# The output projection of a two-layer decoder trunk, split by rows and threaded between the attention heads

## The reference

```python
D_MODEL, SEQ, DEPTH = 2048, 512, 2          # batch 1
# layer 0: S5 state-space mixer (1024) | FoX attention, 8 heads of 128 | memory attention, 4 heads
# layer 1: latent attention MLA, 8 heads | sparse attention NSA, 8 heads | memory attention, 4 heads
for layer in range(DEPTH):
    xn = rms_norm(h, norm_g[layer])
    mem_kv = mem_n @ mem_w_kv[layer]
    mixed = even_layer(xn, mem_kv, ...) if layer % 2 == 0 else odd_layer(xn, mem_kv, ...)
    h = h + (mixed @ w_out[layer]).astype(h.dtype)      # (512, 2560) @ (2560, 2048)
return rms_norm(h, final_norm_g)

# attention, per head: s = q k^T * scale (+ bias); p = softmax(s); o = p v; y = o * silu(gate)
# NSA, per head: three softmaxes (selected 512 keys, window 512 keys, compressed 31 keys),
#   each weighted by its own sigmoid gate, their outputs summed
```

## Time and profile before

| | |
|---|---|
| three executions | 2541.16, 2548.64, 2548.69 us |
| profiled execution, its span | 2541.77 us, 2540.2 us |
| PE, busy | 2366.3 us (93%), 11912 matmuls |
| DVE, ACT, POOL, busy | 1009.8, 831.7, 348.4 us (40%, 33%, 14%) |
| chain that ended last | PE 86%, DVE 5%, issue 3%, DMA 2%, ACT 2% |
| OUT0, OUT1 | 1021.0 to 1240.4 us, 2292.9 to 2512.9 us |
| FOX, MEM0 | 908.5 to 979, 979 to 1021 us |
| MLA, NSA, MEM1 | 2000.6 to 2093, 2103.2 to 2245.3, 2245.3 to 2292.9 us |

### The profile page before, as it was taken

The page is one execution under the profiler, slowest core; times in us unless marked ns, Lnnn a source line. Parts: engine busy times, 40 slices in busy tenths (PEclk is TensorE's granted clock), DMA queues, the critical chain, the costliest instruction groups (busy, mean ns, idle before and its releaser), DMA issues.

```text
span 2540.2 us, 31542 instructions
## 1 busy us (share of the span) xinstructions
PE 2366.3 (93%) x11912; PEld 1913.8 (75%) x11912; DVE 1009.8 (40%) x1863; ACT 831.7 (33%) x1481; POOL 348.4 (14%) x593
## 2 busy tenths in 40 slices
PE   5999999999999887999799999999989997869995
PEld 5888888888888666788687778888868666657884
DVE  4532444544422376322433432222162267853322
ACT  5432233333324244222322322223233345642221
POOL 7404111122100012000100010000001441110000
PEclk9999999999999998999899999999999899989998
DMA  9544444334344333432343454434247434415231
GB/s 255 186 133 127 115 116 126 109 111 125 105 139 143 109 129 95 174 100 93 116 128 119 137 162 138 129 111 132 85 155 230 150 95 151 149 51 190 92 99 66
DMA packets 151623, 328.55 MB, mean 129 GB/s; under 512 B 19623, under 2 KB 21959, under 8 KB 148563
## 3 DMA queue, kind: packets, MB, share of 16 engines
q1 hardware_dynamic: 102016, 186.41, 24.7%
q0 software_dynamic: 29824, 102.61, 12.5%
q10 hardware_dynamic: 19667, 37.95, 4.0%
HBM read 271.49 MB, written 55.43 MB: 129 GB/s over the span
## 4 chain that ended last, share of the span: by engine, by line
PE 86%; DVE 5%; issue 3%; DMA 2%; ACT 2%; POOL 1%; DVEq 0%; ACTq 0%; POOLq 0%; SPq 0%
PE PS L195 72%; PE PS L1258 3%; PE PS L1713 1%; PE PS L1235 1%; PE PS L1840 1%; PE PS L1738 1%; PE PS L1433 1%; DMA wraw<-in_mem_w_kv_dram 1%; PE PS L927 1%; PE PS L923 1%; DMA S<-vmD 1%; PE PS L1734 1%; PE PS L1551 1%; DVE PS L1191 1%; PE PS L391 1%
## 5 line engine op out<-in xcount | busy, mean ns | idle before, releaser
L195 PE MATMUL PS<-A,wsp 128*128 128x512 f32 (+3 forms) x5808 | 1316.3, 386 | 25.1 <-DVE wsp L172 18.0
L195 PEld LDWEIGHTS PS<-A,wsp 128*128 128x128 f32 (+2 forms) x5808 | 1058.2, 188 | 250.3 <-issue 27.2
L172 DVE TENSOR_TENSOR wsp<-wraw,wsp 128x1024 fp32r<-128x1024 f32 (+2 forms) x366 | 432.1, 1186 | 1228.4 <-ACT wsp L168 1227.7
L168 ACT ACTIVATE wsp<-wraw 128x1024 fp32r<-128x1024 f32 (+2 forms) x366 | 373.1, 1024 | 1156.6 <-PE PS L195 1105.7
L195 PE MATMUL PS<-wsp,A 128*128 128x512 f32 x2496 | 575.6, 393 | 12.2 <-issue 6.3
L195 PEld LDWEIGHTS PS<-wsp,A 128*128 128x128 f32 x2496 | 472.6, 190 | 111.9 <-issue 10.0
L1258 PE MATMUL PS<-S 128*128 128x128 f32 x832 | 133.9, 289 | 13.2 <-ACT S L1243 12.9
L246 ACT ACTIVATE stage<-PS 128x512 f32<-128x512 f32 (+1 forms) x150 | 86.2, 587 | 140.6 <-PE PS L195 134.4
L1258 PEld LDWEIGHTS PS<-S 128*128 128x128 f32 x832 | 113.4, 200 | 22.6 <-ACT S L1243 13.2
L1210 ACT ACTIVATE S<-PS,stats 128x512 f32<-128x512 f32 (+3 forms) x192 | 91.7, 478 | 85.1 <-DVE stats L1200 54.1
L1243 ACT ACTIVATE S<-PS 128x512 f32<-128x512 f32 (+3 forms) x192 | 76.1, 396 | 85.2 <-PE PS L1235 84.1
(11 more groups left out here) (284 smaller groups left out, 1620.5 us busy)
## 6 DMA issues: line engine op xcount, KB each, us to landing
wraw<-in_even_w_in_dram SPq DMA_DIRECT2D x112, 512.0 KB, 3.7
wraw<-in_odd_w_in_dram SPq DMA_DIRECT2D x104, 512.0 KB, 3.6
wraw<-in_w_out_dram SPq DMA_DIRECT2D x80, 512.0 KB, 3.6
wraw<-in_mem_w_kv_dram SPq DMA_DIRECT2D x32, 512.0 KB, 4.4
yO<-stage ACTq DMA_DIRECT2D x13, 1024.0 KB
yE<-stage ACTq DMA_DIRECT2D x12, 1024.0 KB
S<-yO POOLq DMA_DIRECT2D x10, 1024.0 KB, 6.9
S<-in_x_dram POOLq DMA_DIRECT2D x8, 1024.0 KB, 11.2
```

Of the source, the lines that this page charges most:

```text
L168: nc.scalar.activation(wsp[:, q, 0, :, 0:j["cols"]], wraw[:, q, :, 0:j["cols"]], ACT.Copy).then_inc(w_hi, 1)
L172: nc.vector.tensor_tensor(wsp[:, q, 1, :, 0:j["cols"]], wraw[:, q, :, 0:j["cols"]], wsp[:, q, 0, :, 0:j["cols"]].bitcast(F32), ALU.subtrac ...
L195: mm = nc.tensor.matmul(dst, lhs, rhs, start=(s == 0 and kk == 0 and i == 0), stop=(s == j["spc"] - 1 and kk == 1 and i == 2))
```

## The change

The 20 row tiles of OUT0 and OUT1 are two jobs now. OUT0A and OUT1A hold the first 8 row tiles (4 chunks of 4 slots, 384 matmuls), whose inputs, the S5 or the MLA tiles, are in `A` before FOX or NSA begins. OUT0B and OUT1B hold the other 12 (4 chunks of 6 slots, 576 matmuls) and stay where OUT was. `Seq` makes one written-out sequence of FOX and MEM0 (48 units) and one of NSA and MEM1 (112 units). MLA stays as it was, in a loop, with its own transposes of the values. Each step of a sequence carries a share of the 384 matmuls, half of it ahead of the scores and half behind the transposes: 8 a step in layer 0, 3 or 4 in layer 1, none in the last one or two steps of a chunk.

```diff
+        OUT0A = job("OUT0A", a["w_out"][0][0:1024, :], 8, 4, mode="T", hi=0, lo=KM)
+        OUT0B = job("OUT0B", a["w_out"][0][1024:MIX, :], KM - 8, 4, mode="T", hi=8, lo=KM + 8, to_stage=False)
+        def pe_seq(pe, t):
+            for x in range(t.steps):
+                m0, m1, m2 = t.cut[x]
+                seq_fill(pe, t, m0, m1)
+                if x < len(t.units):
+                    seq_scores(pe, t, x)
+                if 0 <= x - LT < len(t.units):
+                    seq_turn(pe, t, x - LT)
+                seq_fill(pe, t, m1, m2)
+                if x >= LV:
+                    seq_values(pe, t, x - LV)
```

```diff
+            if x >= 2:
+                pe.wait_ge(a_ex, U - 1)
+            u["score"](pe, PS[:, 4 + x % 2, :]).then_inc(a_sc, 1)
```

```diff
+        def seq_resid(act, t, x):
+            for c, e in enumerate(t.chunk_end):
+                if x == e + 2:
+                    act_store(act, j, c)
+                if x == e + 4 and c < 3:
+                    seq_resid_load(act, t, c + 1)
+        def seq_add(dve, t, c):
+            dve.wait_ge(resid_in, 16 * (4 * t.l + c + 1))
+            for f in range(4):
+                ...
+                nc.vector.tensor_tensor(stage[:, f, :], PS[:, f, :], stage[:, f, :], ALU.add).then_inc(banks_free, 1)
```

```diff
-                nc.vector.scalar_tensor_tensor(bank, bank, t.scale, u["bias"](...)[:, 0:w], ALU.mult, ALU.add).then_inc(t.mx0, 1)
-                nc.vector.tensor_reduce(stats[:, 4 + c:5 + c], PS[:, SB[x % 4], 0:w], AX, ALU.max, negate=True).then_inc(t.mx, 1)
+                nc.vector.tensor_tensor_reduce(bank, bank, u["bias"], -1.0, 3e38, ALU.add, ALU.min, accum_out=top).then_inc(a_mx, 1)
```

More of the change, by code:

```diff
@@ L157, in sp_slot @@
                 return
+            if j is O1 and isinstance(c, int) and c in (5, 6):
+                for half in range(2):
+                    sp.dma_start(wraw[:, q, :, 256 * half:256 * half + 256],
+                                 j["w"][:, 2 * s:2 * s + 2, ds(3648 + 512 * half + 256 * (c - 5), 256)]).then_inc(w_loaded[q], 16)
+                return
             sp.dma_start(wraw[:, q, :, 0:j["cols"]],
@@ L1172, in pe_scores @@
         def pe_scores(pe, t, b, x):
-            if t is FOX and x == 2 and b is t.b0:
-                pe.wait_ge(banks_free, GLU["bank0"] + 8)
             u = unit(t, x)
@@ new lines, in seq_split @@
+        def seq_split(eng, slot_fn, t, slots):
+            j = t.fill
+            for slot in slots:
+                n = j["slot0"] + slot
+                slot_fn(eng, n, n % RAW, n // RAW)
+        def pe_seq(pe, t):
[9 more added lines that the diff above has]
+                    seq_values(pe, t, x - LV)
@@ new lines, in seq_values @@
+        def seq_values(pe, t, x):
+            u, U = t.units[x], t.u0 + x
+            if u["k"] == 0:
+                pe.wait_ge(a_vld[u["r"]], t.vld0 + u["vld"])
+                pe.wait_ge(a_fin0, t.h0 + u["H"])
+            pe.wait_ge(a_ev, U + 1)
+            i = u["i"]
+            for j_ in range(u["nb"]):
+                mm = nc.tensor.matmul(PS[:, 7, i * P:i * P + P], u["v"](j_), seqT[x % 2][:, j_ * P:j_ * P + P],
+                                      start=(j_ == 0 and u["first"]), stop=(j_ == u["nb"] - 1 and u["last"]))
+            mm.then_inc(a_pv, 1)
@@ new lines, in act_seq @@
+        def act_seq(act, t):
+            seq_resid_load(act, t, 0)
+            for x in range(t.steps):
+                seq_resid(act, t, x)
+                seq_split(act, lambda e, n, q, r: act_slot(e, t.fill, n, q, r, False), t, [n for n in range(4, N_FILL) if t.pe_end[n - 4] + 1 == x])
+                if 0 <= x - LT < len(t.units):
+                    seq_turned(act, t, x - LT)
+                if x < len(t.units):
+                    seq_exp(act, t, x)
+            for x in range(t.steps, t.steps + 4):
+                seq_resid(act, t, x)
@@ new lines, in dve_seq @@
+        def dve_seq(dve, t):
+            j = t.fill
+            for x in range(t.steps + 2):
+                if x - LV in t.end:
+                    seq_finish(dve, t, t.end.index(x - LV))
+                for c, e in enumerate(t.chunk_end):
+                    if x == e + 1:
+                        seq_add(dve, t, c)
+                seq_split(dve, lambda e, n, q, r: dve_slot(e, j, n, q), t, [n for n in range(4, N_FILL) if t.pe_end[n - 4] + 1 == x])
+                if x < len(t.units):
+                    seq_max(dve, t, x)
+                if 0 <= x - 1 < len(t.units):
+                    seq_norm(dve, t, x - 1)
@@ L2105, in _ @@
                 pe_chunk(pe, O1, c, lambda s: pe_t5(pe, 8 * (c - 1) + s))
-            with pe.Fori(5, 12) as c:
+            for c in range(5, 12):
                 pe_chunk(pe, O1, c)
@@ L2122, in _ @@
             pe.wait_ge(MLA.fin, MLA.done)
-            pe_att(pe, NSA)
-            pe_att(pe, MEM1)
-            pe.wait_ge(MEM1.fin, MEM1.done)
+            pe_seq(pe, SEQ1)
+            pe.wait_ge(a_fin, MLA.done + HEADS0)
             for c in range(4):
-                pe_chunk(pe, OUT1, c)
+                pe_chunk(pe, OUT1B, c)
         @block.vector
```

555 lines of the change are left out of this document (359 added, 196 removed).

## The result

The changed kernel takes 2457.78 us (median of four, 2450.32 to 2459.41), the kernel before 2545.71 (four, 2541.16 to 2548.69). The ratio is 0.9659, 95% interval 0.9643 to 0.9675. The forecast was 2462, range 2436 to 2496.

A forecast was written before the change was run, and what follows sets the result against it. PE's work plus its waits was taken to bound the kernel. Gains of 29.8 us in layer 0 and 50.1 in layer 1, together 79.9 off the profiled 2541.8, gave 2461.9, predicted as 2462, range 2436 to 2496.

The forecast's parts named there:

- Layer 0: From 908.5 to 1240.4: 285.1 us of PE work plus waits makes 302.1 instead of 331.9, a gain of 29.8.
- the start: Start of layer 0: PE waits 7.2 us for the first exponential, then 2 us for a lower clock.
- Layer 1: From 2093.0 to 2512.9: 342.5 us of PE work plus waits makes 369.8 instead of 419.9, a gain of 50.1.
- MLA's lateness: Layer 1, MLA's start: four DVE slots ahead of its first maximum make it about 1.2 us later.
- three chunk ends: Layer 1's heads: adds and ACT's wait for a store (4.8 us) show about 2 us each; together 12, bounds 0 to 28.
- changing between the kinds of matmul: Threaded heads: 0.03 us a group, 3.1 us for layer 0's 104 groups, 5.8 for layer 1's 192.
- What costs nothing: DVE in FOX and NSA: one-instruction maximum between 0.70 and 1.39 us, taken as 0.9; DVE stays below PE at either bound.
- rival 1: Heads' scores: two score banks bind through the exponential; 0.2 us lost in each of 112 steps, 22 us, 2484; chance 0.17.
- 2: Threaded heads: changing between matmul kinds costs 0.2 us a group, 50 us more, 2512; chance 0.06.
- 3: Threaded heads: the clock falls; 364 us at 0.85 add 64 us, 2526; chance 0.05.
- 4: Threaded heads: slower than before, PE's in-order stream exposes each unit's round trip; 0.9 us a step, 144 us, 2606; chance 0.06.
- 5: Threaded heads: moved matmuls fill nothing, since what PE waits for comes later by as much; about 2541, no change; chance 0.04.

The follow-up runs named there:

- the start experiment: Changed kernel, in layer 0 the first moved matmul no longer waiting for all sigmoids and three of the first four slots prepared a step later: 2454.46 us, ratio 0.9655.
- The unthreaded kernel: Changed kernel with all moved matmuls run behind the last head, chunk by chunk, none beside the heads: 2490.69 us, ratio 0.9791 to the kernel before.
- the first execution: The changed kernel as first measured, against the kernel before: median 2457.78 us, ratio 0.9659; its profiled execution took 2457.88 us.
- the repeat: The changed kernel measured once more without any edit: 2456.03 us, ratio 0.9659 to the kernel before.
- the kernels with spread adds: Changed kernel, VectorE's four chunk-end adds over two steps, residual loaded later: both layers 2452.55 us; layer 1, first three chunks only, 2444.67 us; also in all edits together.
- all edits together: Changed kernel with layer 0's earlier start, layer 1's late residual and spread adds, and weight loads held until MLA's end: 2441.13 us, ratio 0.9605.

## Why the prediction was right, step by step

**Bound and method.** PE's work plus PE's waits described the time: the chain is 90% PE, and counting the work in starts gave heads at 5.86 instead of 6.03 and B jobs of 130.9 and 132.4 instead of 131.6.

**Layer 0, 302.1 forecast, 294.9 measured.** The terms that were too large: the start (9.2 forecast; 3.7 until the first fill from 908.5 on and 2.7 of slow clock behind it make 6.4), work of the heads (1.4), OUT0B (0.7), and chunk ends with changing cost, 4.6 forecast, 2.3 left over. The cause at the start was another too: a wait for banks that the last sigmoid had to leave. That the third score stood within 1 us of the forecast shows why it did not matter; DVE's clean-up sets both, as the start experiment showed.

**Layer 1, 369.8 forecast, 375.0 measured.** The first fill stands at 2060.90, 2.6 later than forecast, 1.2 having been put on MLA's lateness; in four executions of the same code M varied by 4.2 us, and 1.2 lies within what they showed (M 0.6 to 4.8 longer than before; up to 8.4 in the other experiments). Fills and heads up to OUT1B took 237.7 instead of 235.9, and OUT1B 0.8 more. The 12 us for three chunk ends agree with the 10 to 12.5 that rearranging them gave, but in part by luck: 4.9 to 7.0 of these are waits of PE, and most of the rest, by the estimate there, is the clock, for which the sum of layer 1 had no term. The store was mis-sized (8.0, 8.0 and 6.0 us beside the other transfers instead of 4.8), the adds were right in kind. The 5.8 us for changing between the kinds of matmul are not there either, so that the sum is nearer than its parts.

**What costs nothing.** This step failed, though the number did not show it. The prediction held that DVE stays below PE at either end of the bounds of the maximum, and so put its cost at nothing; at 1.39 us it costs 13.7. That the number came out is owed to the instruction taking 0.84, near the 0.9 taken. It is rival 1's mechanism, the chain through two banks of scores, and its price at the upper bound belonged among the terms; the range held it only because it took in most of rival 1.

**Why it gained.** The prediction added work and left-over waits, and let the fills cover layer 1's 3.7 us a head of waits. It counts the end state and not the way there, so it cannot see what removed the waits. The unthreaded kernel shows that many were gone without any fill. N falls from 186.5 to 148.3: 17.7 of these 38.2 us are the waits for the memory heads' loads, 7.0 the 64 transposes of values at 0.11. F falls from 106.3 to 85.4: 10.6 of these 20.9 are the same waits, 3.1 waits for FOX's loads, 3.5 the 32 transposes. The other 13.5 and 3.7 belong to the new order of steps, the banks and the shorter maximum together, which were not taken apart further (in the kernel before, the first two scores of FOX also stand ahead of F). Not all waits were gone: 148.3 is 25.1 above the prediction's 123.2 of work. Threading itself fills 15.5 us in layer 0; in layer 1 it gives 2.5 net of its own chunk ends, 13.5 once these are spread; and it spares 9.4 us of chunks with no head beside them in each layer.

**Rivals.** 1: with the one-instruction maximum PE's waits for the exponential are 5.5 us in layer 1 and 0.4 in layer 0, not 22; its mechanism shows at two instructions. 2: no changing cost (5.86 a head; one group a step changes nothing). 3: the granted clock was 0.98 and 0.97 in the threaded stretches, so they did not run at 0.85. The Trainium skill, "TensorE: Matmul & The Clock Gate", in its section "A second HAM failure mode: psum-queue depth-cycling", tells of a kernel whose clock swings because of small idles between groups of matmuls. Here the trace does not show that between the groups; the falls in the heads stand behind single idles of 1.4 to 3.5 us. 4 and 5: excluded by 0.9659.

## What to carry to other kernels

Moving ready work into a chain's waits pays by the waits that are left once the loads are early. Measure the kernel without the moved work first: here early loads had already removed 28 us of waits for the memory heads alone. With an order of fixed places, look at the few steps where something is added for one step only (a chunk's adds, a queue that waits for a store): spreading them gave 10 to 12.5 us here, nearly as much as the one-pass maximum. An engine that is three quarters busy can still cost time when it stands in a chain with two buffers.

## What the hardware showed that I had not expected

The clock after an idle of the same length differs between executions of the same code. At the first chunk's end PE idled 2.63 us in all of them. Of the first execution and of the repeat:

```profile
2118.72 1.81 PE L1513 MATMUL PS<-S 128*128 128x128 f32 x8 [2.63 <-issue]
2120.18 1.20 PE L212 MATMUL PS<-wsp,A 128*128 128x512 f32 x2
```

```profile
2116.58 1.13 PE L1513 MATMUL PS<-S 128*128 128x128 f32 x8 [2.63 <-issue]
2117.46 0.70 PE L212 MATMUL PS<-wsp,A 128*128 128x512 f32 x2
```

The five microseconds behind it, in the same two:

```profile
2119.00:2124.00 5.00, 5.00 (x26) 4.50 (x25) 2.02 (x10) 1.00 (x5) 0.00 (x0) 0.66 0.89 303
```

```profile
2117.00:2122.00 5.00, 5.00 (x33) 4.27 (x32) 2.87 (x13) 1.00 (x5) 0.00 (x0) 1.00 0.90 317
```

The granted clock is 0.66 in one, a mixture of its two levels (1.2 and 2.4 GHz), and 1.00 in the other. Of the six executions whose heads of layer 1 are this code, the four in which it fell here have N at 231.9, 232.3, 233.5 and 234.5 us, the two in which it did not 228.6 and 230.5. Not all of that is this fall: in those two it fell at later idles instead (0.70 and 0.67 over the 5 us behind one of 1.53 us), and three of the four have a later wait of 3.1 to 3.2 us that the two do not have.

A shorter idle is no safe bound either. In the kernels with spread adds the idle at the first chunk's end is 1.44 us. The clock stayed at 1.00 behind it in two executions, and fell in the one of all edits together:

```profile
2112.20 1.50 PE L1513 MATMUL PS<-S 128*128 128x128 f32 x8 [1.44 <-issue]
```

```profile
2112.50:2117.50 5.00, 5.00 (x26) 4.49 (x25) 3.21 (x12) 1.00 (x5) 0.00 (x0) 0.66 0.93 336
```

What decides between the two I did not find out. Fewer idles give the clock fewer occasions to fall, which fits that removing 7.0 us of waits gave more than 7, and that one kernel's times spread over 10 us; neither was tested by itself.
